# Neighbourhood and dilated attention as one software pipeline, with the dilated heads issued in pairs

## The reference, cut to what matters

```python
out_na = neighbourhood_attention(qa, ka, va, na_rel_bias[i])     # 8 heads of 64
...
for g, (window, dilation) in enumerate(((128, 1), (512, 4), (2048, 16))):   # 4 heads in each group
    o_g, lse_g = dilated_window_attention(qd[:, :, g], kd[:, :, g], vd[:, :, g], window, dilation)
    outs.append(o_g)
    lses.append(lse_g)
wts = jax.nn.softmax(jnp.stack(lses, axis=2), axis=2)
out_dil = jnp.sum(wts[..., None] * jnp.stack(outs, axis=2).astype(jnp.float32), axis=2)
...
merged = (jax.nn.sigmoid(gate_na) * (out_na @ w_branch_na[i])
          + jax.nn.sigmoid(gate_dil) * (out_dil @ w_branch_dil[i]))
```

## Time and profile before

| | us |
|---|---|
| runs timed | 3108.01, 3100.19, 3078.86 |
| median | 3100.19 |
| the profiled execution | 3077.99 |
| its span in the profile | 3076.0 |
| TensorE busy | 3044.3 (99%) |
| VectorE busy | 1732.1 (56%) |
| ScalarE busy | 1272.7 (41%) |

### The profile page before, as it was taken

One profiled execution on the slowest core, in us unless ns is written; L12 is line 12 of the kernel. 1 busy time (PEld: TensorE's weight loads), 2 busy tenths in 40 slices (PEclk: granted clock), 3 DMA queues, 4 the chain that ended last, 5 costly groups with the idle time before them and its releaser, 6 DMA issues.

```text
span 3076.0 us, 40846 instructions
## 1 busy us (share of the span) xinstructions
PE 3044.3 (99%) x15304; PEld 2607.0 (85%) x15304; DVE 1732.1 (56%) x3009; ACT 1272.7 (41%) x2057; POOL 1398.3 (45%) x727
## 2 busy tenths in 40 slices
PE   9999999999999999999999999999999999999998
PEld 6787888888888888899999998878888889888886
DVE  6836436998999910138888875364211337641122
ACT  5445334333777733333333334454333334543331
POOL 4530344344434444567777602454444434344442
PEclk9999999999999999999999999999999999999999
DMA  3240232344477775679999973313333322123332
GB/s 126 71 149 15 83 103 92 96 144 144 138 205 203 207 210 166 205 249 362 370 367 372 369 255 102 104 42 109 97 96 96 107 71 76 43 93 98 100 97 82
DMA packets 323267, 470.24 MB, mean 153 GB/s; under 512 B 120464, under 2 KB 227856, under 8 KB 322464
## 3 DMA queue, kind: packets, MB, share of 16 engines
q1 hardware_dynamic: 300576, 400.83, 40.7%
q0 software_dynamic: 22528, 67.19, 5.9%
HBM read 405.03 MB, written 60.82 MB: 151 GB/s over the span
## 4 chain that ended last, share of the span: by engine, by line
PE 97%; DVE 2%; DMA 1%; issue 0%; ACT 0%; SPq 0%; POOL 0%; DVEq 0%
PE pb L776 29%; PE pb L778 29%; PE pb L777 29%; PE pb L1117 1%; PE pb L1386 1%; PE pb L1010 1%; PE pb L875 1%; PE pb L988 1%; PE pb L1067 0%; PE pb L1172 0%; PE pb L998 0%; PE pb L990 0%; PE pb L901 0%; PE pb L1254 0%; PE pb L938 0%
## 5 line engine op out<-in xcount | busy, mean ns | idle before, releaser
L646 POOL TENSOR_TENSOR s_over<-s_ring,s_rhigh 128x1024 fp32r<-128x1024 f32 x401 | 987.2, 2464 | 1479.6 <-ACT s_rhigh L1495 1479.1
L1495 ACT ACTIVATE s_rhigh<-s_ring 128x1024 fp32r<-128x1024 f32 x525 | 556.0, 1060 | 1119.4 <-DMA s_ring<-w 516.1
L776 PE MATMUL pb<-s_over,s_rhigh 128*128 128x512 f32 (+1 forms) x2384 | 874.7, 367 | 0.6 <-DVE s_over L2318 0.5
L778 PE MATMUL pb<-s_over,s_over 128*128 128x512 f32 (+1 forms) x2384 | 871.4, 366 | 0.0
L777 PE MATMUL pb<-s_over,s_rhigh 128*128 128x512 f32 (+1 forms) x2384 | 871.2, 365 | 0.0
L776 PE MATMUL pb<-s_hS,s_rhigh 128*128 128x512 f32 (+1 forms) x1664 | 656.3, 394 | 3.5 <-DVE s_hS L2623 2.5
L778 PE MATMUL pb<-s_hS,s_over 128*128 128x512 f32 (+1 forms) x1672 | 646.3, 387 | 0.0
L777 PE MATMUL pb<-s_hS,s_rhigh 128*128 128x512 f32 (+1 forms) x1664 | 643.1, 386 | 0.0
L776 PEld LDWEIGHTS pb<-s_over,s_rhigh 128*128 128x128 f32 x2384 | 447.5, 188 | 55.0 <-issue 1.0
L778 PEld LDWEIGHTS pb<-s_over,s_over 128*128 128x128 f32 x2384 | 447.5, 188 | 53.5
L777 PEld LDWEIGHTS pb<-s_over,s_rhigh 128*128 128x128 f32 x2384 | 447.6, 188 | 53.3 <-issue 1.0
(11 more groups left out here) (297 smaller groups left out, 3270.1 us busy)
## 6 DMA issues: line engine op xcount, KB each, us to landing
s_ring<-w SPq DMA_DIRECT2D x272, 512.0 KB, 3.5
s_ring<-eu SPq DMA_DIRECT2D x128, 512.0 KB, 4.1
s_ring<-ev SPq DMA_DIRECT2D x128, 512.0 KB, 6.2
acts<-s_arena SPq DMA_DIRECT2D x128, 256.0 KB, 4.1
s_arena<-acts SPq DMA_DIRECT2D x128, 192.0 KB, 5.3
s_arena<-gates SPq DMA_DIRECT2D x128, 192.0 KB, 6.6
gates<-s_arena SPq DMA_DIRECT2D x36, 512.0 KB, 5.7
gates<-s_arena SPq DMA_DIRECT2D x6, 1024.0 KB, 7.6
```

Of the source, the lines that this page charges most:

```text
L646: gp.tensor_tensor(rlow[:, s, :, :], ring[:, s, :, :], rhigh[:, s, :, :].bitcast(F32), ALU.subtract).then_inc(S("w_split"), 1)
L776: mm(dst, a_high, b_high, start=start, stop=False)
L778: return mm(dst, a_low, b_high, start=False, stop=stop)
L1495: sc.activation(rhigh[:, s, :, :], ring[:, s, :, :], ACT.Copy).then_inc(S("w_high"), 1)
```

## The change

The three loops now run through all 32 steps, without an end and a new start between the attentions. On TensorE the dilated steps are taken in pairs: `dil_scores(k)` issues the scores of the heads 2k and 2k+1 in turn, and `dil_out(k)` their outputs in turn. The dilated scores have four buffers in SBUF (`sq`, `std` and the two of `sc1`), and the transposed probabilities four (`pt2`, over the finished `qkna`). VectorE copies the output of a dilated head five steps behind its maxima instead of three. The transfer of the mask `dil0` starts four steps earlier and has its own place. The linear of T_GATE+1 moves from behind the attention into its last turns.

```diff
-            dil0 = Area(at_bias).take(4, T)
+            dil0 = Area(at_bias + 8 * 256).take(4, T)
...
+        sc2 = [v.rearrange("p a b -> p (a b)")[:, 0:768] for v in (sq, std)] + [sc1[:, b, :] for b in range(2)]
+        pt2 = [Area(768 * b).take(768) for b in range(4)]
...
-            sp.wait_ge(S("at_max"), 16)
+            sp.wait_ge(S("at_max"), 12)
             sp.dma_start(dil0, a["c_dil0"]).then_inc(S("masks_in"), 16)
...
-            attention(16, 0, na_scores, na_turn, na_out, na_beside, na_ahead)
-            pe.wait_ge(S("at_out"), 16)
+            def dil_scores(k):
+                u, c = divmod(k, 2)
+                pe.wait_ge(S("at_max"), DIL0 + 2 * k)
+                heads = [slice(e * HD, (e + 1) * HD) for e in range(2)]
+                for e in range(2):
+                    mm(pb[:, e * 2, :], qkd[heads[e], c, u:T:4], qkd[heads[e], 6 + c, :], start=True, stop=True)
                 for g in (1, 2):
+                    for e in range(2):
+                        m = mm(pb[:, e * 2 + 1, (g - 1) * P:g * P], qkd[heads[e], 2 * g + c, u:T:4],
+                               qkd[heads[e], 6 + 2 * g + c, u:T:4], start=True, stop=True)
+                        if g == 2:
+                            m.then_inc(S("at_scores"), 1)
             def dil_turn(s):
-                if s >= 1:
-                    pe.wait_ge(S("at_pt"), DIL0 + s)
+                pe.wait_ge(S("at_prob"), DIL0 + s + 1)
+                pe.wait_ge(S("at_pt"), DIL0 + s)
...
+            def dil_out(k):
+                u, c = divmod(k, 2)
+                pe.wait_ge(S("at_pt"), DIL0 + 2 * k + 2)
+                pe.wait_ge(S("at_out"), DIL0 + 2 * k)
                 for b in range(6):
+                    for e in range(2):
+                        s, h = 2 * k + e, 2 * c + e
...
+                        m = mm(pb[e * HD:(e + 1) * HD, 6 + s % 2, 0:P], v, pt2[s % 4][:, b * P:(b + 1) * P],
+                               start=b == 0, stop=b == 5)
+                        if b == 5:
+                            m.then_inc(S("at_pv"), 1)
...
+            dil_scores(0)
+            pe.wait_ge(S("at_prob"), DIL0)
+            na_turn(DIL0 - 1).then_inc(S("at_turned"), 1)
+            for i in range(DIL0, DIL0 + 2):
+                pe.wait_ge(S("at_pt"), i - 1)
+                pe.wait_ge(S("at_out"), i - 3)
+                na_out(i - 2).then_inc(S("at_pv"), 1)
+            for k in range(10):
+                if 1 <= k <= 8:
+                    dil_turn(2 * k - 2)
+                if k < 7:
+                    dil_scores(k + 1)
+                elif k == 7:
+                    pe.wait_ge(S("at_max"), DIL0 + 16)
+                    linear(T_GATE, 0)
+                elif k == 8:
+                    linear(T_GATE + 1, 1)
+                if 1 <= k <= 8:
+                    dil_turn(2 * k - 1)
+                if k >= 2:
+                    dil_out(k - 2)
...
-                linear(T_GATE + 3 * o + 1, b0 + 1)
+                if o >= 1:
+                    linear(T_GATE + 3 * o + 1, b0 + 1)
...
-            attention(16, DIL0, dil_exp, dil_pt, lambda i: parts(T_GATE + 3) if i == 4 else None)
+                if s >= 4:
+                    sc.wait_ge(S("at_pv"), DIL0 + s - 3)
+                return sc.activation(pt2[s % 4], src, ACT.Copy)
+            attention(32, 0, lambda s: na_exp(s) if s < DIL0 else dil_exp(s - DIL0),
+                      lambda s: na_pt(s) if s < DIL0 else dil_pt(s - DIL0),
+                      lambda i: parts(T_GATE + 3) if i == DIL0 + 4 else None,
+                      between=lambda i: value(18 + i) if i < 2 else None)
...
-                for i in range(n + 3):
+                for i in range(n + (5 if s0 == 0 else 3)):
                     if i < n:
                         ve.wait_ge(S("at_scores"), s0 + i + 1)
...
-                    if i >= 3:
-                        ve.wait_ge(S("at_pv"), s0 + i - 2)
-                        outp(i - 3).then_inc(S("at_out"), 1)
+                    late = 5 if s0 == 0 and i >= DIL0 + 5 else 3
+                    if i >= late and not (s0 == 0 and DIL0 + 3 <= i < DIL0 + 5):
+                        ve.wait_ge(S("at_pv"), s0 + i - late + 1)
+                        outp(i - late).then_inc(S("at_out"), 1)
...
+                if s >= 2:
+                    ve.wait_ge(S("at_turned"), DIL0 + max(s - 3, 0))
```

More of the change, by code:

```diff
@@ new lines, in _ @@
+            na_scores(0).then_inc(S("at_scores"), 1)
+            for i in range(DIL0):
+                if i + 1 < DIL0:
+                    if i >= 1:
+                        pe.wait_ge(S("at_max"), i)
+                    na_scores(i + 1).then_inc(S("at_scores"), 1)
+                na_ahead(i)
+                if i >= 1:
+                    pe.wait_ge(S("at_prob"), i)
+                    na_turn(i - 1).then_inc(S("at_turned"), 1)
+                na_beside(i)
+                if i >= 2:
+                    pe.wait_ge(S("at_pt"), i - 1)
+                    if i >= 4:
+                        pe.wait_ge(S("at_out"), i - 3)
+                    na_out(i - 2).then_inc(S("at_pv"), 1)
@@ L1608, in na_exp, with na_pt @@
                 return m
-            attention(16, 0, na_exp,
-                      lambda s: sc.activation(pt1[:, s % 2, 0:512], pb[:, 4 + s % 2, :], ACT.Copy),
-                      between=lambda i: value(18 + i) if i < 2 else None)
+            def na_pt(s):
+                return sc.activation(pt1[:, s % 2, 0:512], pb[:, 4 + s % 2, :], ACT.Copy)
             def dil_exp(s):
-                v = sc1[:, s % 2, :]
+                v = sc2[s % 4]
                 return sc.activation(v, v, ACT.Exp, bias=st1[:, s % 2, 3:4], accum_out=st1[:, s % 2, 4:5])
@@ L2052, in attention @@
             def attention(n, s0, buffers, smax, norm_p, outp, between=None):
-                for i in range(n + 3):
+                for i in range(n + (5 if s0 == 0 else 3)):
                     if i < n:
                         ve.wait_ge(S("at_scores"), s0 + i + 1)
-                        if i >= buffers:
+                        if i >= buffers and s0 + i not in range(DIL0, DIFF0):
                             ve.wait_ge(S("at_turned"), s0 + i - buffers + 1)
@@ L2132, in dil_outp @@
                 return ve.tensor_copy(dilT[e, h // 2, u:T:4], pb[e, 6 + s % 2, 0:P])
-            attention(16, DIL0, 2, dil_max, dil_prob, dil_outp)
+            attention(32, 0, 3, lambda s: na_max(s) if s < DIL0 else dil_max(s - DIL0),
+                      lambda s: na_prob(s) if s < DIL0 else dil_prob(s - DIL0),
+                      lambda s: na_outp(s) if s < DIL0 else dil_outp(s - DIL0))
             ve.wait_ge(S("at_out"), DIL0 + 16)
```

40 lines of the change are left out of this document (10 added, 30 removed).

## The result

The changed kernel takes 3118.8 us (median of 18 runs, 3112.8 to 3124.0). The kernel before, run beside it 18 times, takes 3105.5 (3078.9 to 3114.6). The ratio is 1.0045, with a 95% interval of 1.0033 to 1.0057: 14 us slower (10 to 18), which is under 1% but clear of the noise. Forecast were 3097 us, in a range of 3062 to 3125, and less than 1% either way with 0.88. The time lies in the range, 22 us above the number.

A forecast was written before the change was run, and what follows sets the result against it. TensorE bounds the kernel; the 28.4 us that pairing frees come back as waits, so the stretch sums to 0, plus 8 us for the clock. From 3089.5, the middle of four runs, that gives 3097 us, range 3062 to 3125.

The forecast's parts named there:

- the stretch: Dilated attention with the neighbourhood's end and gate linears: 83.0 us before and after, sum 0 (-2 to +2), clock +8.
- the base of the sum: Whole kernel: sum made against the profiled 3078.0 us; 3089.5, middle of four runs, plus 8 gave 3097.
- the count and length of the clock's drops: Dilated rounds: five of the pauses each drop the granted clock to half for 3.4 us, costing +8 us.
- Pairs overlap at one head's price: TensorE, dilated attention: a pair's scores 2.11 us and outputs 1.47; eight pairs release 28.4 us.
- The wait: Dilated loop: VectorE's copy waits behind scores its maxima release; 8.5 us a pair, TensorE idle 3.3, against 8.7 before.
- the copy doesn't hold VectorE: Rival, dilated loop: rounds of 5.9 us, eight save 22 us, giving 3056 or 3067; chance 8%.
- The clock stays low: Rival: TensorE runs the whole stretch at half clock, +36 to +47 us, 3114 to 3125 or 3126 to 3137; chance 8%.
- Edits at no cost: Earlier mask transfer, and gate weights fetched and split by ScalarE and POOL: nothing, or 1 or 2 us once if cover fell short.
- My upper bound, +14: Dilated rounds: cost in us if all eight pauses drop the clock; the lower bound, none dropping it, is 0.
- the first three rounds: Start of the dilated pairs, without a dilated copy and shorter: some 6.4, 5.8 and 6.8 us, 19.0 in all.
- the tail: End of the stretch: two linears 10.9, transposes 2.4, outputs 4.4, two waits of 0.9, 19.5 us, plus 1.4 for the split.
- the splitting's pause: Behind the attention: TensorE waits 1.4 us for the first split, no longer covered by the linear of T_GATE+1.

The follow-up runs named there:

- the filled pauses: The changed kernel with 24 extra unused 256-column matmuls on TensorE in each pause ahead of the scores, k from 2 to 7: 3111.2 us, 1.0024 of before.
- The later copy: The changed kernel with only VectorE's copy of an output moved to six steps behind the maxima in place of five: 3100.8 us, 0.9991 of before.
- the changed order: The changed kernel with only TensorE's order in a round changed, outputs of pair k-2 ahead of scores of pair k+1: 3092.3 us, 0.9947 of before.
- the two largest taken out together: The changed kernel with pauses filled by extra matmuls and the fourth gate tile's rounding moved to dilated step 15: 3102.1 us, 0.9981 of before.
- the mended order: The changed kernel with outputs issued ahead of the next scores and VectorE's copy four steps behind the maxima: 3088.4 us, 0.9953 of before.
- heads singly: The kernel with outputs ahead of scores and copy four steps behind, a pair's heads issued one after the other: 3097.8 us, 0.9971 of before.

## Why the prediction was wrong

Of the 22 us by which the median missed 3097, 16 are the base and 6 the stretch (13 to 14 us slower by the runs, for +8). Three steps failed: the base of the sum, the term for GpSimd's work, and the count and length of the clock's drops.

**What held.** Pairs overlap at one head's price: 1.25 us for four L986 passes, 1.53 for 24 L1014. (The prediction's reading of the neighbourhood's outputs was loose: twelve in 1.53 are 0.13 us each, and eight 1.02, so 0.67 is two thirds of them and not half. The measured pair settles it.) The wait is where the prediction put it and as long: TensorE's pause was 3.14 us (forecast 3.3), and the round at full clock 8.40 (forecast 8.5), shown by the filled pauses. The later copy and the changed order, which touch nothing but that loop, took 20 and 18 us off the mark. Of the rivals, "the copy doesn't hold VectorE" falls, yet its price was sound: its 5.9 us a round is what the kernel has (5.79) once the order is mended. "The clock stays low" came half true: 44.4 of the 75 us from 253 to 329 ran at half clock, but it came back in between each time.

**The base**, "The middle of the four is 3089.5; with +8 I forecast 3097", is the step that cost most. The profiled run of before, 3078.0, is the only one of 13 profiles without the piece at half clock in the mixture-of-experts stage, and I took the middle of four runs, 3089.5, where 18 give 3105.5. So the working said 8 us slower, while the number stood 3 us under the 3100.2 that the runs timed had for before. From 3105.5 the same working gives 3113.5.

**A term put at nothing** is GpSimd beside VectorE. Under "Edits at no cost" the prediction set the work of ScalarE and POOL on the gate's weights at nothing because its next due time was far off; but its price isn't lateness, it is what it does to VectorE. The same stall stood in the trace of before, where it cost nothing, since TensorE was the bound. The change made VectorE part of the path and did not ask what else slows VectorE. Measured: 3.1 us in its round, up to 4.8 us on the mark.

**The clock**: "I take five, +8 us". Forecast were five pieces of 3.4 us, 17 us at half clock. There were seven in 253 to 329 us, 44.4 us in all, and no round of the eight was spared. I had counted pauses and taken 3.4 us for each; three lasted 6.8 us and one 13.7, and the row I went by, could not show how drops follow each other when the next pause comes 7 us later. By the experiments the clock costs 9 to 11 us: 8.6 measured, and about 1.9 that the extra matmuls cost themselves in the third round. So the +8 was 1 to 3 us short although the half clock was over twice as long; what the 13.7 us of it that the filled kernel keeps are worth was not measured. My upper bound, +14, was not passed.

Against the sum's terms: the first three rounds took 21.3 us (248.15 to 269.45) for a forecast 19.0, the fourth, with GpSimd in it, 13.0 for 9.1, the next four (282.42 to 323.05) 40.6 for 34.0, and the tail (to 346.89) 23.8 for 20.9. With the pauses filled that tail took 21.2, so nearly all of its excess is the clock's too. In it the splitting's pause was 2.40 us for 1.4, mostly because the copies' 0.8 stand in it too; moving the tile back behind the attention gave 0.3.

The sum of these on the stretch: clock 9 to 11, GpSimd 3 to 5, the tile's cover under 1, and about nothing from the loop's waits against the old order, as forecast, which gives 12 to 17 for a measured 15.1 or 11.8 by the two profiles of before. The parts overlap (a shorter pause also keeps the clock), so they are not exact shares, and the two largest taken out together left 1.8 to 5.1 us on the mark.

What sets off the slow piece in the mixture-of-experts stage was not tried and stays open: TensorE has many short waits there that the profile shows as issue, and they begin ahead of the half clock, so the clock may follow from them.

## What to carry to other kernels

When a change frees an engine, follow one turn of the new loop through every engine in order, and ask of each in-order wait whether the work it waits for stands behind work that it releases. Here swapping two blocks and moving one copy a step turned a round of 8.4 us, 10 with the clock, into 5.8. Once a second engine is on the path, everything that slows it counts, so look in the old trace for stalls of it that used to be free. A pause of TensorE that comes back each round, here 3.1 us in 10, should be priced with the clock's fall in every round, and with longer falls than a single pause shows. And a base should come from many runs and more than one profile: it was the largest part of the miss.

## What the runs showed of the hardware

- The granted clock fell with TensorE hardly idle: 0.63 in 254 to 268 us of the second profile of before, with 13.67 of 14 us busy, where the first profile of the same kernel has 1.00 with 13.43 busy. In the kernel with the mended order it was at half for 3.4 us from 253 us on, and for 20.5 with the same order and heads singly, where TensorE was busier in 254 to 268 us (13.01 of 14 us against 11.79). Why is open.
- Repeated pauses of 3.14 us in rounds of 10 us gave half clock in each round, repeated ones of 1.94 in rounds of 7.2 in one of the last three, and ones of 1.56 in rounds of 6.8 in none of the last three.
- A VectorE operation of one element a partition took 1.32 us beside GpSimd's 128x1024 subtraction, 0.16 otherwise; the maxima L2113, which read PSUM, took their 0.68 beside it.
- Matmuls of two heads on the two halves of the array's rows overlap in part even when all of one head's are issued first: 3.18 us for two heads' scores, 2.11 issued in turn.
